# Taking the context half of the second mixer into the first layer's gather pass

## What is computed

```python
def gla_mixer(h_lat, h_ctx, ...):
    qc, kc, vc, rc, gc = gla_project(h_ctx, ...)
    ql, kl, vl, rl, gll = gla_project(h_lat, ...)
    o_cf, s_f = gla_chunked(qc, kc, vc, gc[:, :, 0], s0)      # s0 = 0
    o_cb, s_b = gla_reverse(qc, kc, vc, gc[:, :, 1], s0)
    o_lf, _ = gla_chunked(ql, kl, vl, gll[:, :, 0], s_f)
    o_lb, _ = gla_reverse(ql, kl, vl, gll[:, :, 1], s_b)
    out_lat = gla_readout(o_lf + o_lb, rl, gn_g, w_out)       # need_ctx_out is False here
```

## Time and profile before

| | us |
|---|---|
| median of 3 runs | 3968.54 (3967.02 to 3970.99) |
| the profiled execution | 3970.53 |
| its span, first to last instruction | 3968.7 |
| PE (TensorE matmul) busy | 3422.8, 86% |
| DVE (VectorE) busy | 1775.7, 45% |
| ACT (ScalarE) busy | 1094.2, 28% |
| POOL (GpSimd) busy | 828.1, 21% |

### The profile page before, as it was taken

One profiled execution on the slowest core, in us unless ns is written; L12 is line 12 of the kernel. 1 busy time (PEld: TensorE's weight loads), 2 busy tenths in 40 slices (PEclk: granted clock), 3 DMA queues, 4 the chain that ended last, 5 costly groups with the idle time before them and its releaser, 6 DMA issues. The chain is left out here.

```text
span 3968.7 us, 36322 instructions
## 1 busy us (share of the span) xinstructions
PE 3422.8 (86%) x11708; PEld 1524.0 (38%) x11708; DVE 1775.7 (45%) x4116; ACT 1094.2 (28%) x2956; POOL 828.1 (21%) x796
## 2 busy tenths in 40 slices
PE   8988999999999986998898777877779977777776
PEld 7635444343444344343353222222234443222222
DVE  0142111111111134676765876676531336667665
ACT  0130111111111111344443444343333003334433
POOL 0010000000000001344443443434400003444442
PEclk9988899999999998999999999999999678999999
DMA  6495799999999924999999999999951007999998
GB/s 269 182 372 215 301 424 420 424 423 421 423 423 421 401 85 159 422 421 421 416 420 420 412 409 421 415 400 421 422 238 56 22 27 307 422 421 421 412 412 341
DMA packets 157189, 1375.18 MB, mean 347 GB/s; under 512 B 18480, under 2 KB 19120, under 8 KB 25594
## 3 DMA queue, kind: packets, MB, share of 16 engines
q0 software_dynamic: 111360, 805.46, 49.0%
q1 hardware_dynamic: 45690, 568.10, 34.9%
HBM read 1372.33 MB, written 1.15 MB: 346 GB/s over the span
## 5 line engine op out<-in xcount | busy, mean ns | idle before, releaser
L2085 PE MATMUL ps<-sb_arena,sb_diag 128*128 128x512 f32 x3072 | 1502.8, 625 | 391.7 <-ACT sb_diag L2066 388.4
L2000 POOL DMA_INDIRECT sb_arena<-in_uv,sb_idx x768 | 815.4, 1062 | 2815.0 <-POOLq L1399 1656.9
L2028 DVE SCALAR_TENSOR_TENSOR sb_arena<-sb_arena,sb_H 128x1024 f32<-128x1024 f32 x768 | 941.0, 1226 | 653.6 <-DMA sb_arena<-in_uv,sb_idx 481.8
L2085 PEld LDWEIGHTS ps<-sb_arena,sb_diag 128*128 128x128 f32 x3072 | 555.9, 194 | 1318.6 <-ACT sb_diag L2066 787.4
L958 PE MATMUL ps<-sb_ring,sb_arena 128*64 128x512 f32 x3072 | 682.6, 597 | 0.0
L2057 ACT ACTIVATE sb_act<-sb_dots 128x1 f32<-128x1 f32 x768 | 155.0, 202 | 1135.9 <-DVE sb_arena L2028 1135.3
L958 PEld LDWEIGHTS ps<-sb_ring,sb_arena 128*64 128x64 f32 x3072 | 212.6, 137 | 442.0 <-issue 438.2
L2066 ACT ACTIVATE sb_diag<-sb_consts,sb_act 128x128 f32<-128x128 f32 x768 | 308.4, 402 | 29.4 <-PE ps L2085 4.5
L1092 DVE TENSOR_SCALAR sb_arena<-ps 128x512 f32<-128x512 f32 x32 | 22.1, 692 | 554.5 <-PE ps L958 554.5
L171 PE MATMUL ps<-sb_ring,sb_arena 128*128 128x512 f32 x576 | 257.7, 607 | 5.6 <-PE ps L171 1.5
L2061 ACT ACTIVATE sb_act<-sb_act,sb_wts 128x1 f32<-128x1 f32 x768 | 226.2, 295 | 24.9
(11 more groups left out here) (261 smaller groups left out, 2207.8 us busy)
## 6 DMA issues: line engine op xcount, KB each, us to landing
sb_ring<-in_moe SPq DMA_DIRECT2D x192, 2048.0 KB, 10.8
sb_ring<-in_w_mod SPq DMA_DIRECT2D x24, 2048.0 KB, 9.2
sb_ring<-in_w_in SPq DMA_DIRECT2D x11, 2048.0 KB, 13.8
sb_ring<-in_a_w_in SPq DMA_DIRECT2D x8, 2048.0 KB, 11.7
sb_ring<-in_w_q SPq DMA_DIRECT2D x6, 2048.0 KB, 11.5
sb_arena<-in_uv,sb_idx POOLq DMA_INDIRECT x768
sb_ring<-in_b_w_in SPq DMA_DIRECT2D x6, 2048.0 KB, 16.4
sb_ring<-in_a_w_out SPq DMA_DIRECT2D x4, 2048.0 KB, 11.1
```

Source lines behind the costliest of these rows:

```text
L2000: pool.indirect_dma_start(uv[n_ % BUFS], None, table, bass.IndirectOffsetOnAxis(m.idx[:, pair % 2, k:k + 1], 0))\
L2028: nc.vector.scalar_tensor_tensor(out=u, in0=u, scalar=1.0, in1=m.H[:, order[i], :], op0=ALU.mult, op1=ALU.mult, accum_out=m.dots[:, n_ % P ...
L2085: last = nc.tensor.matmul(out[h], m.diag[n_ % DIAGS], uv[b][:, D + h * 512:D + (h + 1) * 512], start=opens, stop=ends)
```

## The change

A class `States` takes over the context half of the GLA mixer. As `Late` does, it hands generators to the three engines, which are run after each slot of `peer` in layer 0, at slots written out by hand (pace 1), in the latent tiles' slots 272 to 476 and in the same PSUM banks 4 to 7.

- Slots 272 to 283: the context tiles are turned into ring slot 3; the low-rank gate input is one product chain for both directions (32 rows, 256 columns).
- Slots 284 to 345: v in half groups of four products (slots 284 and 290, 296 and 302, and again 32 later), and one gate product behind each pair, with Exp and Ln on ScalarE five slots behind it. For this SP loads value chunks 1 and 2 one after the other into ring slot 0, before key chunk 0 goes there as it did before.
- Slots 348 to 371: k in half groups. Slot 372: decays (16 products of two columns); 375, 380, 385, 390: suffix sums, with an Exp on ScalarE three slots later and `k_end` on VectorE five slots later.
- Slots 398 to 473: 32 products k^T v, two every five slots, added to states that lie in `m.X[:, 2:4]`.

In `gla`, `tiles` is 2 in place of 4: 10 projection jobs of 512 columns in place of 16, four gate products and four suffix products in place of eight, half the decay products, and four state steps per head, the first from the state left by `States`, with three updates in place of seven. Its buffers move from ring slots 2 and 3 to the arena. The gate weights have a buffer of their own and are loaded in the pass; those of both directions now lie in one matrix of 33 rows with zeros where the other direction's are. The loads of value chunks 1 and 2 in `gla` stay, since the latent tiles need them.

```diff
+class States:
+        for h in range(GH):
+            for s in range(4):
+                at["kv", h, s] = 398 + 5 * (4 * h + s)
...
+    def sync(self, sp):
+        sp.dma_start(m.w_gl, d["b_w_gl"]).then_inc(M("gate_in"), 16)
+        sp.dma_start(m.w_gate, d["b_w_gate"]).then_inc(M("gate_in"), 16)
+        sp.wait_ge(M("idx_ready"), 2 * PAIRS)
+        for n in range(2):
+            if n:
+                sp.wait_ge(M("states_v_used"), n)
+            sp.dma_start(m.ring[:, 0, :], d["b_w_in"][1 + n]).then_inc(M("states_v_in"), 16)
+        sp.wait_ge(M("states_v_used"), 2)
+        ring.load(sp, ring.at["b_w_in"] + 1)
...
+    def tensor(self, pe):
+        for n in range(2):
+            for t in range(TT):
+                where = plan["v", n, t]
+                for half in range(2):
+                    yield at["v", n, t] + 6 * half
+                    pe.wait_ge(M("states_v_in"), 16 * (n + 1))
+                    half_products(where, half, t, self.w_v)
+                part = self.parts[2 * n + t]
+                yield at["z", part]
+                if t == TT - 1:
+                    pe.wait_ge(M(f"bank_full{where[0]}"), where[1] + 1)
+                    pe.sem_inc(M("states_v_used"), 1)
...
+    def scalar(self, act):
+        def logs(n):
+            act.wait_ge(M("states_abs"), n + 1)
+            nc.scalar.activation(self.a, self.a, ACT.Exp, scale=-1.0).then_inc(M("states_exp"), 1)
+            act.wait_ge(M("states_exp"), n + 1)
+            nc.scalar.activation(self.a, self.a, ACT.Ln, bias=1.0).then_inc(M("states_log"), 1)
...
 def peer(nc, d, m, M, banks, ring, layer, first, out_dram=None):
-            beside = Beside(late.tensor(pe) if layer == 0 else iter(()), LATE_PACE)
+            beside = [Beside(late.tensor(pe), LATE_PACE), Beside(states.tensor(pe))] if layer == 0 else []
...
-                beside.upto(n)
+                for work in beside:
+                    work.upto(n)
...
 def gla(nc, d, m, M, banks, ring):
-    tiles = 4
+    tiles = TT
...
-                for s in range(8):
+                for s in range(4):
                     for j in range(2):
                         t, c = steps[j][s]
                         rows_ = slice(c * CH, (c + 1) * CH)
-                        if s >= 4:
...
+                        if s:
+                            pe.wait_ge(M(f"state_ready{j}"), 3 * h + s)
+                        last = nc.tensor.matmul(m.ps[rows_, where[0], t * DV:(t + 1) * DV],
+                                                q_in[:, j, h, t * P + c * CH:t * P + (c + 1) * CH], state(h, j, s),
+                                                start=False, stop=s == 3, skip_group_check=True)
...
-                for s in range(7):
+                for s in range(3):
```

More of the change, by code:

```diff
@@ L2005, in _ @@
             step = Chain(M, dve, "dve_step")
-            beside = Beside(late.vector(dve, step) if layer == 0 else iter(()), LATE_PACE)
+            beside = [Beside(late.vector(dve, step), LATE_PACE), Beside(states.vector(dve, step))] if layer == 0 else []
             def finish(i):
@@ L2042, in _ @@
         def _(act):
-            beside = Beside(late.scalar(act) if layer == 0 else iter(()), LATE_PACE)
+            beside = [Beside(late.scalar(act), LATE_PACE), Beside(states.scalar(act))] if layer == 0 else []
             for n, (i, q, k) in enumerate(slots):
@@ L2091, in _ @@
                         pe.sem_inc(M(f"bank_full{sums[t, h][0]}"), 1)
-                beside.upto(n)
+                for work in beside:
+                    work.upto(n)
 def gla(nc, d, m, M, banks, ring):
-    tiles = 4
-    hT = m.part(0, KT, tiles * P)
+    tiles = TT
+    hT = m.part(0, KT, T)
     k_end = m.part(0, tiles, 2, GH * DK)
+    yT = m.part(0, KT, T)
+    q_in = m.part(2048, 2, GH, T)
     v = m.part(4096, tiles, D)
+    new_hT = m.part(4096, KT, T)
+    k_in = m.part(6144, 2, GH, T)
     g = m.part(8192, tiles, 2, GH * DK)
+    o = m.part(8192, TT, D)
+    r = m.part(10240, TT, D)
     k = m.part(12288, tiles, GH * DK)
-    o = m.part(12288, TT, D)
-    r = m.part(14336, TT, D)
-    yT = m.part(0, KT, T)
+    S = m.part(13312, 2, 2, DV)
+    att = m.part(14336, 2, 512)
+    early_ab = m.part(14336, 2, 512)
+    ab = m.part(15360, 2, 512)
     H = m.H[:, :, :].rearrange("p a b -> p (a b)")
@@ L2129, in gla @@
     m.norms += TT * GH + TT
-    new_hT = m.part(4096, KT, T)
-    ends = [m.part(8192 + i * D, D) for i in range(4)] + [m.part(2048, D)]
+    ends = [m.part(at, D) for at in (2048, 3072, 6144, 7168, 12288)]
     base = M.n.get("h_ready_now", 0)
@@ L2184, in _ @@
                     pe.wait_ge(M(f"bank_free{hs[t, n][0]}"), hs[t, n][1] + 1)
[L2186 to L2193 removed]
+            where = proj["gl"]
+            banks.wait_free(pe, where)
+            banks.fill(products(nc, m.ps[0:2 * RANK, where[0], 0:T], [(w_gl[:, c, :], hT[:, c, :]) for c in range(KT)]), where)
             for n, job in enumerate(jobs):
@@ L2546, in pair_heads, with gate_rows @@
     return np.moveaxis(w, -1, axis)
+def gate_rows(w, bias):
+    rows = np.zeros((2 * RANK + 1, 2, GH * DK), np.float32)
+    for j in range(2):
+        rows[RANK * j:RANK * (j + 1), j, :] = w[j]
+        rows[2 * RANK, j, :] = bias[j]
+    return rows
 def layout(i):
```

263 lines of the change are left out of this document (197 added, 66 removed).

## The result

The changed kernel took 3876.9 us, the median of four runs (3875.9 to 3878.8), against 3968.2 for the kernel before on the same chip (four runs, 3967.0 to 3971.0). The ratio is 0.9769, 95% interval 0.9753 to 0.9786.

The account below looks back on a forecast made before the run. The first layer's gather pass was taken as bound by DMA bytes, the second mixer by TensorE. Mixer savings of 84.5 us, less 10.6 of bytes and 15 of stalls, gave -58.9 us: 3910 us, range 3893 to 3930.

Parts of the forecast that it names:

- projections and gates: Mixer: 16 projection jobs become 10, 42.6 us saved, and eight gate jobs become four, 4.4 saved.
- the suffixes: Mixer: four of eight suffix products go, 3.5 us saved.
- the decay: Mixer: the decay products, 10.09 us, halve, 5.0 us saved.
- The bytes: First layer's gather pass: 4.46 MB more loads, unhidden, displace gathers at 421 GB/s and cost 10.6 us.
- the head loop's term: Mixer's head loop: each head's opening (first k^T v products, updates, wait) goes, mean 5.7 us, four times, 22.8 saved.
- The stalls' term: First layer's gather pass: side work stalls the gathers, 15 us lost in sum, ends 0 and 35.
- up to about 5.5 us costs nothing; what is beyond is lost: Gather pass: POOL pauses up to about 5.5 us are free with eight buffers, anything longer is lost time.
- The four gate pieces: Gather pass: ScalarE's Exp and Ln, three table loads and two passes, 5.1 us each; 5.4 us lost in all.
- Turning and gate input: Mixer: half the turning of h goes, 2.7 us saved, and half the low-rank gate input's products and columns, 3.5 saved.
- Stalls are absorbed: Rival for the gather pass: the eight buffers take every piece; 3895 us, 15%.
- The head loop gives back only half, because VectorE ends last: Rival for the head loop: VectorE's norms, masking and first state step end last; 11 us less, 3921 us, 9%.
- The slower case: Rival for the gather pass: TensorE stays at 1.2 GHz, 1.0 us lost per slot, about 4100 us over all slots; 2%.

Follow-up runs that it names:

- one chunk: Changed kernel with one value chunk loaded in the pass in place of two, both halves of v taken from it: 3873.1 us, 0.9762.
- the kernel without the work: Changed kernel with the context half left out of the pass, its pieces on all engines and its two value chunk loads: 3863.9 us, 0.9740.
- the equal passes: Eight profiled kernels, the changed one among them, with the same pass and differences only behind it: passes of 1365.4 to 1368.9 us, mean 1366.9.
- the kernel with tables alone: Changed kernel without the context half's work, but with ScalarE's Exp and Ln and their table loads on scratch data at the same slots: 3865.1 us, 0.9742.
- the reordered version: Changed kernel with the next head's scores and masking moved behind the first state step: 3873.0 us, 0.9769; second set 3875.2 us, 0.9756.
- products only: Changed kernel plus each head's eight removed k^T v products, with one-column copies for the state updates and no wait for them: 3888.1 us, 0.9798.
- 128 rows: Changed kernel with each head's removed products, updates and wait put back, the products taking 128 rows in place of 64: 3900.4 us, 0.9829.

## Why the prediction was wrong

**Right, within 1.2 us.** The projections and gates (47.5 for 47.0), the suffixes (3.6 for 3.5) and the decay (6.1 for 5.0). kT waits for nothing that can be seen, and nothing behind the head loop or in the second pass moved. The bytes agree with displacement: 3 to 4 us for one chunk of 5.0. By the sum's own structure (a TensorE-bound mixer paying a byte-bound pass) the result is what it said.

**The step that failed: the head loop's term.** The prediction took the opening's own time, 5.7 us four times, 22.8 in all, and left the steps behind it at "a granted clock of 0.50, 1.2 GHz, ... before and after". The loop gave back 43.1. The opening's own time was right (23.6 us for the four), but taking it away also gave the steps 2.4 GHz in most of the loop: pairs of 0.65 and 0.70 us instead of 1.11 and 1.22. That is the other 19.5 us. Putting the opening back took all of it away again (92.5). The rows to see it in stood there: the earlier trace rows has an idle time of 1.25 us right at each opening's end and the earlier trace rows a clock of 0.50 with TensorE never idle; I read the second as a property of the steps, and it was one of what came ahead of them. The trace of before also had a warning that I passed over: in its last head, the first q S behind such a wait, at 3185.60, takes 0.65 us.

**The stalls' term was too large.** 15 us were forecast and 2 to 4 came: 14.4 less the bytes' 10.6 against the kernel before, 13.1 less 10.0 against the kernel without the work, each 1.2 less by the mean of the equal passes. The failed step is "up to about 5.5 us costs nothing; what is beyond is lost". A pause of 6.03 us beside 393 GB/s was read as the pause's price; pauses of 7.0 us cost nothing in the kernel with tables alone. The four gate pieces, for which 5.4 were put in, leave 419 to 424 GB/s in their windows. What the decay, the suffixes at the latent finish and the state steps cost one by one no run here tells apart; together with all else they are the 2 to 4 us.

**Smaller.** Turning and gate input gave 4.3 for 6.2, since the shorter gate input runs at a clock of 0.62 where it had 1.00 before; that the small turning products ahead of it are the reason is argued only. 3.4 us came in the start, which the change does not touch.

With the two terms as measured the sum would be 3909.6 - (43.1 - 22.8) - (15 - 3.8) = 3878.1 us, 1.2 above the median. So close a fit is partly luck, since the smaller misses (3.4 us in the start, 1.9 the other way in turning and gate input, 1.1 in the decay) offset one another in part.

**The rivals.** "Stalls are absorbed" came nearly true. "The head loop gives back only half, because VectorE ends last" did not: VectorE is late twice, by 1.1 us, in a loop that runs mostly at twice the clock, and the reordered version leaves one wait of 0.3 us. The slower case, a pass stuck at 1.2 GHz, did not show: the clock's slices over the pass are at 0.8 or above.

The Trainium skill (ScalarE: Activation LUTs, What ACT_TABLE_LOAD costs) puts a drain of about 1.38 us behind each load. The trace after disagrees as the one before did: the load at 2373.78 takes 1.28 us and its ACTIVATE stands at 2375.08, with the next load at 2375.73. The extra 30 us of ScalarE's time that the prediction worked out from that page did not come.

**Open.** Why one head of the four, the third, falls to 0.50 even in the changed kernel, with products only and with 128 rows, is not settled; the reordered version, which has no such wait there, does not show it. That the wait of 1.1 us is the reason is not shown either, since the second head has the same wait and stays at 1.00. The opening with its short wait and no products was not measured.

## What to carry to other kernels

The cost of a block of small products on TensorE is its own time plus what it does to the clock of the work behind it: where a stretch stands at 1.2 GHz while TensorE is never idle, look at what ended just ahead of it, and cost its removal at both clocks (here 22.8 and 43 us). In this pass, bound by bytes and with eight buffers, single pauses of the issuing engine of up to 7 us were not a price; compare GB/s around a pause with a kernel that lacks the suspected work before putting a loss down to it, and profile the same pass more than once: here equal passes differ by 3.5 us. What this pass did charge, in the main, is bytes.

## What the runs showed of the hardware

- Products of 64 rows and products of 128 rows, with otherwise the same queue and the same wait of 1.24 us behind them, leave TensorE at 1.2 GHz in all four heads and at 2.4 GHz in three of four: 92.5 and 72.7 us for the same head loop.
- POOL's pauses of 7.01 and 7.02 us between gathers left their 25 us windows at 421 GB/s. A gather takes 13.8 us from issue to landing (median, 2200 to 2800 us); that those in flight cover the pause is argued, not tried.
- Two plain loads of 2048 KB landed in 12.0 and 11.6 us in the middle of a stream of gathers at a DMA share of 1.01, and took no longer than the 12.2 us of before.
